# The gate products of a mixing layer: one block instead of five, low parts on GpSimd, four high buffers, gates through DRAM

## The chip, the cores and the metric

One core of a Trainium2 chip. The metric is the device time of one execution in microseconds; before the change the median of three runs is 4073.41 us (4073.11 to 4075.11). The profiled execution took 4088.57 us, of which its records span 4086.9.

## What is computed

The kernel runs two transformer blocks on 256 tokens of width 2048 in float32. The first ends in a layer of product-key experts, whose rows are gathered from DRAM. The second is a mixing layer and a feed-forward layer. The change is in the mixing layer of the second block:

```python
proj = h @ w_in                     # 2048 x (10240 + 16 + 3 * 2048); the last 6144 columns are the gates
o_sb  = stick_breaking_attention(rms(q_sb), rms(k_sb), v_sb)     # 6 heads of 128
o_dil = dilated_mixture(rms(q_dil), rms(k_dil), v_dil, slopes)   # 6 heads, three dilations, softmax over them
log_a = log_sigmoid(a_gla @ w_gla_a + b_gla_a) / 16
o_gla = rms(gla(q_gla, k_gla, v_gla, log_a)) * silu(r_gla)       # 4 heads, gated linear attention
g = sigmoid(gate_cols.reshape(b, t, 3, 2048))
y = g[:, :, 0] * (o_sb @ w_br_sb) + g[:, :, 1] * (o_dil @ w_br_dil) + g[:, :, 2] * (o_gla @ w_br_gla)
x = x + gate1 * (y @ w_out)
```

## The kernel before

**Slabs.** Every weight matrix is streamed from DRAM in slabs of 512 rows by 512 columns (1 MB, `ring`, four slots, loaded by SP's queue in the order of the program). A float32 product is made of three products of rounded operands: ScalarE writes a slab's rounded value (`high_part`, L336, 128x2048) into one of two buffers `slab_high`, a second engine subtracts it from the slab (`low_part`, L343), and TensorE multiplies high by high, low by high and high by low (24 matmuls a slab). For the slabs of the gates and of the branches the low part goes back into the slab's own ring slot (`ring_low`; `is_in_place`), so that slot is free only when TensorE has used the slab (`slot_free`). Semaphores count slabs: `landed`, `high_done`, `low_done`, `slabs_used`.

**Gates between the attention's products.** The 48 gate slabs (12 blocks of 512 columns, four slabs each) are independent of the attention. Five blocks of instructions in turn hold the attention (heads L1847, stick-breaking L1950, dilated L2066, gated linear L2221, branches L2431), and at chosen places of each engine's program the helpers `gate_loads`, `gate_highs`, `gate_lows` and `gate_slabs` put in the gate slabs up to a given number. TensorE makes 8 slabs by the end of the heads, 14 by the end of the stick-breaking part, 21, and 36; the last 12 follow at the head of the branch block. VectorE does all the attention's arithmetic and the low parts of the gate slabs, one at a time between its steps (`then` waits for the step before). Products of the gates go to the banks 6 and 7. After each fourth slab ScalarE takes them out with a sigmoid (L1808) into `staged`; SP writes nine of the twelve blocks to DRAM (`gate_rows`, L1789) and reads them back in three pieces (L2436); the last three stay in SBUF.

**The gated linear attention** goes over eight levels (`for lv in range(LV + 1)`, L2399): TensorE makes a level's products from `qe` and `ke`; VectorE scales these for the next level (L2289, L2290), masks and adds this level's products (L2306 to L2312), and forms the next exponents (L2283, L2285), of which ScalarE takes the exponential (L2354). TensorE made one gate slab between two levels.

**Branches.** 16 slabs, whose products with the attention's outputs are multiplied with the gates (L2489) and summed (L2494) into `y`.

Before this part stands the section `MIX` (the first 10240 columns of `w_in`), whose left operand is made by `final` and `normed` from the residual `res`. After it `transposed` and `gated_residual("mixer", ...)` multiply `y` with `w_out` and add to `res` (L2573). The gathers of the experts (L1668), long before, are issued by GpSimd, which copies 8 row numbers (L1661) for every 8 gathers, while VectorE works through the rows (L1515, L1529).

Of the kernel before, what the change touches and what calls it, by code (L numbers as in the profile page):

```python
# [9 lines left out]
F32 = mybir.dt.float32  # L10
# [19 lines left out]
def build(nc, a, out):  # L30
# [39 lines left out]
    with ctx:  # L70
# [39 lines left out]
        res_, _ = place_at("res", TT * D)  # L110
# [19 lines left out]
        low = low_[:, :].rearrange("p (s k n) -> p s k n", s=PARTS, k=KS)  # L130
        res, nat = view(res_[:, :], [TT, D]), view(nat_[:, :], [TT, D])
# [108 lines left out]

        def split_index(g):

            return g - whole_before[g]
# [84 lines left out]
        def high_part(act, g, i=None):  # L328

            n, up = split_index(g), 0 if i is None else i * 8  # L330
            act.wait_ge(landed[g % SLOTS], reach[g] if i is None else i * 32 + reach[g])
            if i is not None:
                act.wait_ge(slabs_used, up + (g - PARTS + 1))
            elif n >= PARTS:
                act.wait_ge(slabs_used, split_slabs[n - PARTS] + 1)  # L335
            nc.scalar.copy(high[:, n % PARTS], ring[:, g % SLOTS]).then_inc(high_done, 1)  # L336

        def low_part(eng, g, i=None):
# [4 lines left out]
            eng.tensor_tensor(dst, ring[:, g % SLOTS], high[:, n % PARTS].bitcast(F32), ALU.subtract)\  # L343
# [1066 lines left out]
        s_hi, s_lo = sem("mix_left_high"), sem("mix_left_low")  # L1410
        s_wa, s_ap = sem("rank_columns_landed"), sem("rank_products")
# [14 lines left out]
        with nc.Block() as block:  # L1426
# [255 lines left out]
            def _(sp):  # L1682
# [15 lines left out]
                sp.dma_start(shift_row, mods[0].rearrange("(k q) -> k q", q=P).partition_broadcast(P)).then_inc(s_shf, 16)  # L1698
                stream(sp, MIX)
                sp.wait_ge(s_wa, 80)  # L1700

# [74 lines left out]
        SPILLED = GATE_BLOCKS - 3  # L1776
        gate_rows = nc.dram_tensor("gate_rows", (SPILLED, P, TT * NB), F32, kind="Internal").ap()
        staged = spare[:, 3 * TT * NB:4 * TT * NB]
        last_gates = view(spare[:, 0:3 * TT * NB], [3, TT, NB])
        s_gate, s_spill = sem("gates_done"), sem("gates_spilled")  # L1780
        at = {"SP": 0, "PE": 0, "ACT": 0, "DVE": 0}

        def gate_loads(sp, end):

            for m in range(at["SP"], end):
                b = m // 4 - 1
                if m % 4 == 0 and 0 <= b < SPILLED:
# [5 lines left out]
        def gate_highs(act, end):  # L1793

            for n in range(at["ACT"], end):
                if n % 4 == 1 and 0 <= n // 4 - 1 < GATE_BLOCKS:
                    sigmoid(act, n // 4 - 1)
                high_part(act, gate0 + n)
            at["ACT"] = end

        def sigmoid(act, b):

            act.wait_ge(slabs_used, gate0 + 4 * b + 4)
            if 0 < b < SPILLED:
                act.wait_ge(s_spill, 16 * b)
            for t in range(TT):
                dst = staged[:, t * NB:(t + 1) * NB] if b < SPILLED else last_gates[:, b - SPILLED, t, :]
# [3 lines left out]
        def gate_lows(dve, end):  # L1811

            for n in range(at["DVE"], end):
                low_part(dve, gate0 + n)
            at["DVE"] = end
# [15 lines left out]
        def in_place_product(g, k, o, lh, ll, first, final):  # L1831

            hi = high[:, split_index(g) % PARTS, k, :]
# [3 lines left out]

        s_hs, s_hr, s_hn = sem("head_step"), sem("head_root"), sem("heads_normed")
# [8 lines left out]
        with nc.Block() as block:  # L1847
            @block.sync
            def _(sp):
                gate_loads(sp, 8)  # L1850

            @block.vector
            def _(dve):
                v = nc.vector
                n = [0]

                def then(ins, mark=None):
                    ins.then_inc(s_hs, 1)
                    n[0] += 1
                    hmarks[mark] = n[0]  # L1860
                    dve.wait_ge(s_hs, n[0])

                def copy_pair(m):
                    dve.wait_ge(s_hT, m + 1)
                    for j in range(2):
                        _, _, dst, hh, gcol = heads[2 * m + j]
                        src = ps[m % 4][:, j * T:(j + 1) * T]
                        if gcol is None:
                            last = v.tensor_scalar(dst[:, hh, :], src, P ** -0.5 if dst is gqT else 1.0, None, ALU.mult)
                        else:  # L1870
                            last = v.tensor_scalar(dst[:, hh, :], src, gains[:, gcol:gcol + 1], None, ALU.mult)
                    last.then_inc(s_hc[1], 1)

                gate_lows(dve, 1)
                copy_pair(1)
                copy_pair(3)
                for t in range(TT):
                    for i, qk in enumerate((sb_qk, dil_qk)):
                        hv = view(qk[:, t, :], [2 * SBH, HD])
                        then(v.tensor_tensor(sq, hv, hv, ALU.mult))  # L1880
                        then(v.tensor_reduce(qk_ss[:, t, i * 2 * SBH:(i + 1) * 2 * SBH], sq, AX, ALU.add))
                        gate_lows(dve, 2 + 2 * t + i)
                then(v.tensor_scalar(qk_ss, qk_ss, 1.0 / HD, EPS, ALU.mult, ALU.add), "ss")
                dve.wait_ge(s_hr, 1)
                then(v.reciprocal(qk_ss, qk_ss))
                for i, qk in enumerate((sb_qk, dil_qk)):
                    for t in range(TT):
# [828 lines left out]
```

## Time and profile before

| | |
|---|---|
| median of 3 runs | 4073.41 us |
| profiled execution, its span | 4088.57 us, 4086.9 us |
| TensorE busy | 2384.8 us, 58% of the span |
| VectorE busy | 2670.7 us, 65% |
| ScalarE busy | 809.8 us, 20% |
| GpSimd busy | 1152.0 us, 28%, nearly all before 2330 us |
| DMA, mean over the span | 252 GB/s |

All times in the views are microseconds from the start of the span unless they are marked ns. PE is TensorE, PEld its weight loads, DVE is VectorE, ACT is ScalarE, POOL is GpSimd, SP the engine that issues the loads. "L343" is a line of the kernel. A matmul's duration overlaps with the next one's; busy time doesn't count the overlap twice. The part that the change touches begins at 2697.5 us, when the first gate slab's high part starts, and ends at 3200.7 us, when the transposes of `y` start.

### The profile page before, as it was taken

The numbers are of one execution on the slowest core, as the hardware profiler recorded it, in microseconds if no ns is written. First come the engines' busy times: TensorE is split into PE (matmuls) and PEld (weight loads), VectorE is DVE, ScalarE is ACT, GpSimd is POOL, SyncE is SP. The second block draws the span as 40 slices with busy tenths as digits, with TensorE's granted clock in tenths as the row PEclk, the third lists the DMA queues.
The fourth block names the chain that finished last, engine by engine and source line by source line (L and its number), as shares of the span: only waits on it lengthen the run. The fifth ranks groups of instructions, "written<-read, shape, count | busy, mean of one in ns | idle before, by whom it ended". The sixth has DMA issues, their size and how long they took to land. (4 is left out here: it accounts for less than half of the span.)

```text
span 4086.9 us, 28912 instructions
## 1 busy us (share of the span) xinstructions
PE 2384.8 (58%) x10296; PEld 1784.6 (44%) x10296; DVE 2670.7 (65%) x2821; ACT 809.8 (20%) x679; POOL 1152.0 (28%) x605
## 2 busy tenths in 40 slices
PE   7798877870000000000000099998879969999999
PEld 4444436640000000000000088886668758888787
DVE  1876645367999988998888844456765544444444
ACT  1000113310000000000000033334433333333333
POOL 0000000005777888888888600000000000000000
PEclk9899978875555555555555599989989989999999
DMA  5255585669999999999999755533446545555554
GB/s 167 103 177 204 176 317 182 218 248 409 402 402 388 391 380 388 374 412 389 373 395 369 309 181 191 193 110 127 130 147 204 184 148 190 188 191 186 182 192 160
DMA packets 332247, 1029.49 MB, mean 252 GB/s; under 512 B 35256, under 2 KB 35768, under 8 KB 264696
## 3 DMA queue, kind: packets, MB, share of 16 engines
q1 hardware_dynamic: 258424, 491.31, 35.6%
q0 software_dynamic: 73728, 536.90, 32.8%
q8 instruction: 61, 1.00, 0.1%
q14 instruction: 34, 0.28, 0.0%
HBM read 1021.28 MB, written 6.86 MB: 252 GB/s over the span
## 5 line engine op out<-in xcount | busy, mean ns | idle before, releaser
L343 DVE TENSOR_TENSOR slab_low<-ring,slab_high 128x2048 fp32r<-128x2048 f32 x240 | 549.7, 2292 | 713.5 <-ACT slab_high L336 713.5
L336 ACT CAST slab_high<-ring 128x2048 fp32r<-128x2048 f32 x304 | 579.5, 1909 | 1051.7 <-PE bank L322 811.8
L1718 PE MATMUL bank<-ident,nat 128*128 128x128 f32 x32 | 8.9, 433 | 1300.7 <-DVE nat L1574 1300.7
L1529 DVE SCALAR_TENSOR_TENSOR res<-pool,res 128x2048 f32<-128x2048 f32 x256 | 603.2, 2356 | 81.1 <-DMA pool<-in_peer_v,small 52.5
L320 PE MATMUL bank<-slab_high,left_high 128*128 128x512 f32 x1568 | 616.3, 393 | 27.8 <-DVE slab_low L343 27.8
L1515 DVE CUSTOM_DVE_ANT_0 pool<-pool,nat 128x2048 f32<-128x2048 f32 x256 | 576.8, 2292 | 62.5 <-DMA pool<-in_peer_u,small 52.7
L321 PE MATMUL bank<-slab_low,left_high 128*128 128x512 f32 x1568 | 614.2, 392 | 0.0
L322 PE MATMUL bank<-slab_high,left_low 128*128 128x512 f32 x1568 | 613.8, 391 | 0.0
L1668 POOL DMA_INDIRECT pool<-in_peer_v,small x256 | 550.6, 2151 | 102.7 <-issue 68.3
L1718 PEld LDWEIGHTS bank<-ident,nat 128*128 128x128 f32 x32 | 5.7, 216 | 1304.6 <-DVE nat L1574 1304.6
L1668 POOL DMA_INDIRECT pool<-in_peer_u,small x256 | 501.6, 1960 | 153.8 <-issue 74.5
L320 PEld LDWEIGHTS bank<-slab_high,left_high 128*128 128x128 f32 x1568 | 297.1, 189 | 90.0 <-DVE slab_low L343 28.8
L322 PEld LDWEIGHTS bank<-slab_high,left_low 128*128 128x128 f32 x1568 | 296.9, 189 | 62.4
L321 PEld LDWEIGHTS bank<-slab_low,left_high 128*128 128x128 f32 x1568 | 297.2, 190 | 61.8
L311 PE MATMUL bank<-ring,left_scratch 128*128 128x512 f32 x640 | 277.9, 595 | 1.0 <-PEq L477 1.0
L1307 POOL IOTA small<- 128x16 f32 x1 | 0.1, 149 | 846.0 <-SPq L1304 846.0
L343 DVE TENSOR_TENSOR ring_low<-ring,slab_high 128x2048 fp32r<-128x2048 f32 x64 | 146.7, 2292 | 101.2 <-ACT slab_high L336 95.9
L1834 PE MATMUL bank<-slab_high,left_high 128*128 128x512 f32 x384 | 160.3, 418 | 55.8 <-DVE ring_low L343 42.9
L311 PEld LDWEIGHTS bank<-ring,left_scratch 128*128 128x128 f32 x640 | 121.7, 191 | 151.1 <-issue 151.1
L396 PE MATMUL bank<-ring,pool 128*32 128x512 f32 x768 | 122.5, 752 | 72.1 <-DMA ring<-in_w_ada 62.5
L1835 PE MATMUL bank<-ring_low,left_high 128*128 128x512 f32 x384 | 155.9, 406 | 0.0
L1836 PE MATMUL bank<-slab_high,left_low 128*128 128x512 f32 x384 | 155.8, 406 | 0.0
(494 smaller groups left out, 2877.8 us busy)
## 6 DMA issues: line engine op xcount, KB each, us to landing
ring<-in_w_in SPq DMA_DIRECT2D x148, 1024.0 KB, 5.1
ring<-in_w_ada SPq DMA_DIRECT2D x96, 1024.0 KB, 7.3
ring<-in_w_ffn_in SPq DMA_DIRECT2D x88, 1024.0 KB, 5.0
ring<-in_w_ffn_out SPq DMA_DIRECT2D x44, 1024.0 KB, 5.0
ring<-in_w_out SPq DMA_DIRECT2D x32, 1024.0 KB, 5.1
ring<-in_peer_wq SPq DMA_DIRECT2D x16, 1024.0 KB, 5.1
ring<-in_w_br_gla SPq DMA_DIRECT2D x8, 1024.0 KB, 5.0
gate_rows<-slab_low_scratch SPq DMA_DIRECT2D x9, 512.0 KB, 5.9
```

The costliest lines, as they stand in the source:

```text
L311: last = nc.tensor.matmul(o, raw_left[:, k0 + k, t * P:(t + 1) * P], ring[:, slot, k, :], start=start and k == 0, stop=stop and k == KS - 1)
L320: nc.tensor.matmul(o, lh, high[:, part, k, :], start=first, stop=False)
L321: nc.tensor.matmul(o, lh, low[:, part, k, :], start=False, stop=False)
L322: last = nc.tensor.matmul(o, ll, high[:, part, k, :], start=False, stop=final)
L336: nc.scalar.copy(high[:, n % PARTS], ring[:, g % SLOTS]).then_inc(high_done, 1)
L343: eng.tensor_tensor(dst, ring[:, g % SLOTS], high[:, n % PARTS].bitcast(F32), ALU.subtract)\
L1515: v.tensor_tensor_reduce(out=rows_[r], in0=rows_[r], in1=nat[:, t, :], scale=1.0, scalar=0.0, op0=ALU.mult, op1=ALU.add, accum_out=dots[:, ...
L1529: v.scalar_tensor_tensor(res[:, t, :], rows_[r], actv[:, t, bass.ds(i * GB + r, 1)], res[:, t, :], ALU.mult, ALU.add).then_inc(s_free, 1)
L1668: g.indirect_dma_start(rows_[r], None, src, bass.IndirectOffsetOnAxis(st[:, r:r + 1], 0))\
L1834: nc.tensor.matmul(o, lh, hi, start=first, stop=False)
L1835: nc.tensor.matmul(o, lh, ring_low[:, g % SLOTS, k, :], start=False, stop=False)
L1836: return nc.tensor.matmul(o, ll, hi, start=False, stop=final)
```

## The change

It leaves the arithmetic as it is, apart from where and when it is done:

- The five blocks become one. What each engine did in them are functions (`heads_on_tensor`, `stick_on_vector`, and so on) that are called in turn; new semaphores (`s_ol`, `s_gol`, waits for `s_hc` and others) replace the ends of the blocks.
- The low parts of all 64 in-place slabs are made by GpSimd (`gate_lows(g, ...)`) instead of VectorE.
- For these slabs there are four high buffers instead of two: the two of `slab_high` and two laid over `res`, which is written to DRAM before the `MIX` slabs and read back in the `mixer` block.
- All 48 gate slabs are made between the attention's products; the table `BEFORE` says how many slabs TensorE has made before each step. ScalarE goes four slabs further (`+ DEEP`) before each of its steps.
- All 12 blocks of gate products go to DRAM, as plain copies of the banks; they come back in four pieces, and the sigmoid is taken then, one of 128x3072 for each.

```diff
+        DEEP = 2 * PARTS
+        def high_of(g):
+            if is_in_place(g):
+                slot = (g - first_slab[GATES]) % DEEP
+                return high[:, slot] if slot < PARTS else over_res[:, slot - PARTS]
+            return high[:, split_index(g) % PARTS]
...
+            elif is_in_place(g) and g - first_slab[GATES] >= DEEP:
+                act.wait_ge(slabs_used, g - DEEP + 1)
+            elif is_in_place(g) and g - first_slab[GATES] >= PARTS:
+                act.wait_ge(s_away, 16)
...
+                sp.wait_ge(s_res, 4 * TT)
+                sp.dma_start(residual_rows, res_[:, :]).then_inc(s_away, 16)
                 stream(sp, MIX)
...
-        SPILLED = GATE_BLOCKS - 3
+        BEFORE = {"h4": 4, "h8": 6, "h12": 8, "sa": 8, "sb": 12, "sc": 16, "da": 16, "db": 20, "dc": 22, "ga": 24,
+                  "gb": 25, "gc": 28, "g1": 28, "g2": 30, "g3": 32, "g4": 34, "g5": 36, "g6": 38, "g7": 40, "g8": 42,
+                  "go": 44, "gt": 46}
...
-            for n in range(at["ACT"], end):
-                if n % 4 == 1 and 0 <= n // 4 - 1 < GATE_BLOCKS:
-                    sigmoid(act, n // 4 - 1)
+            for n in range(at["ACT"], min(end, IN_PLACE)):
+                if n % 4 == 3 and 0 <= n // 4 - 1 < GATE_BLOCKS:
+                    take_gate(act, n // 4 - 1)
                 high_part(act, gate0 + n)
...
-                last = nc.scalar.activation(dst, ps[6 + t][:, :], ACT.Sigmoid)
+                last = nc.scalar.copy(staged[:, t * NB:(t + 1) * NB], ps[6 + t][:, :])
...
+            for m in (4, 8, 12):
+                gate_highs(act, BEFORE[f"h{m}"] + DEEP)
+                copy_pair(m)
+                copy_pair(m + 2)
...
+        def stick_on_scalar(act):
+            gate_highs(act, BEFORE["sa"] + DEEP)
+            act.wait_ge(s_ss, sm["abs"])
...
+            gate_highs(act, BEFORE["sc"] + DEEP)
+            for h in range(SBH):
+                act.wait_ge(s_so, h + 1)
+                nc.scalar.copy(oTh[:, h, :], ps[h][:, 0:T]).then_inc(s_oc, 1)
...
+        def gla_on_gpsimd(g):
+            gate_lows(g, BEFORE["db"])
+            g.wait_ge(s_mk, 4)
+            g.wait_ge(s_so, SBH)
+            g.wait_ge(s_ds, dk["max"])
+            g.memset(upto[:, :], 1.0).then_inc(s_gi, 1)
...
+            for lv in range(1, LV + 1):
+                gate_highs(act, BEFORE[f"g{max(lv - 1, 1)}"] + DEEP)
+                act.wait_ge(s_gs, gm[f"diff{lv}"])
+                nc.scalar.activation(ee, ee, ACT.Exp).then_inc(s_gf, 1)
...
+            gate_loads(sp, B0 + 1)
+            sp.wait_ge(s_gs, gm["out"])
+            for n in (0, 1, 3):
+                read_back(n)
+            sp.wait_ge(s_gT2, 4)
+            read_back(2)
+            gate_loads(sp, IN_PLACE)
...
+        def branch_on_scalar(act):
+            gate_highs(act, B0 + 4)
+            for nb in range(OB):
+                act.wait_ge(s_back[nb], 16)
+                nc.scalar.activation(sg[nb], sg[nb], ACT.Sigmoid).then_inc(s_sg, 1)
+                gate_highs(act, B0 + 4 * nb + 8)
+
+        def branch_on_gpsimd(g):
+            gate_lows(g, IN_PLACE)
...
+                    if residual_away:
+                        sp.dma_start(res_[:, :], residual_rows).then_inc(s_away, 16)
```

## Rows read from the trace of the kernel before

**Rows 1.** Busy times by stretch: busy us (count) of each engine, TensorE's granted clock, DMA.

```profile
2697.50:2759.60 62.10, 55.45 (x256) 45.88 (x256) 47.66 (x39) 27.97 (x32) 0.00 (x0) 0.93 0.42 137
2759.60:2821.70 62.10, 49.10 (x252) 41.16 (x253) 35.51 (x32) 25.93 (x21) 0.89 (x4) 0.92 0.35 113
2821.70:2887.00 65.30, 54.17 (x246) 44.47 (x246) 40.90 (x62) 26.83 (x43) 0.53 (x2) 0.92 0.40 129
2887.00:2911.70 24.70, 23.14 (x102) 18.12 (x102) 14.18 (x17) 13.76 (x11) 0.87 (x4) 0.93 0.53 169
2911.70:2994.00 82.30, 64.28 (x328) 54.09 (x328) 78.91 (x77) 27.25 (x23) 0.00 (x0) 0.96 0.33 106
2994.00:3039.00 45.00, 31.32 (x137) 25.34 (x136) 26.78 (x22) 18.38 (x17) 0.00 (x0) 0.87 0.38 118
3039.00:3110.20 71.20, 68.59 (x289) 55.92 (x290) 27.51 (x12) 22.93 (x15) 0.00 (x0) 0.96 0.69 243
3110.20:3200.70 90.50, 87.32 (x385) 71.82 (x384) 59.03 (x47) 29.64 (x17) 0.00 (x0) 1.00 0.57 192
```

**Rows 2.** TensorE's waits from 2697 to 3201: us in total, times, longest.

```profile
PE bank L1834 <- DVE ring_low L343: 42.9, 13, 10.0
PE bank L1834 <- ACT slab_low_scratch L1808: 9.5, 6, 2.9
PE bank L1834 <- PEq L2221: 3.4, 1, 3.4
```

**Rows 3.** Groups of instructions, 2697 to 3110: low and high parts, exponentials and their tables.

```profile
L343 DVE TENSOR_TENSOR ring_low<-ring,slab_high 128x2048 fp32r<-128x2048 f32 x49 | 112.3, 2292 | 72.5 <-ACT slab_high L336 67.4 <-PEq L2221 4.3
...
L336 ACT CAST slab_high<-ring 128x2048 fp32r<-128x2048 f32 x49 | 93.1, 1905 | 181.8 <-PE bank L1836 157.7 <-PEq L1426 24.0
...
L2354 ACT ACTIVATE slab_low_scratch<-slab_low_scratch 128x1024 f32<-128x1024 f32 x8 | 8.5, 1057 | 4.5 <-DVE slab_low_scratch L2285 4.5
...
L2354 ACT ACT_TABLE_LOAD x2 | 2.6, 1283 | 0.0
```

**Rows 4.** DMA issues, 2690 to 3215: size of one, us to landing.

```profile
ring<-in_w_in SPq DMA_DIRECT2D x44, 1024.0 KB, 5.0
...
pool<-gate_rows SPq DMA_DIRECT2D x3, 1536.0 KB, 8.6
```

**Rows 5.** Busy times while two read-backs and a slab are under way.

```profile
3052.00:3056.00 4.00, 4.00 (x19) 3.31 (x18) 0.97 (x1) 1.91 (x1) 0.00 (x0) 1.00 1.03 417
```

**Rows 6.** GpSimd's copy of 8 numbers, and two of the 64 beside VectorE's timeline.

```profile
L1661 POOL COPY small<-pool x64: 187/1770/2183, 919.0 to 2298.0; 128x8 uint32 x62, 128x8 uint32<-128x8 uint32 x2
...
2032.47 2.35 DVE L1529 SCALAR_TENSOR_TENSOR res<-pool,res 128x2048 f32<-128x2048 f32 x1 [0.43 <-DMA pool<-in_peer_v,small]
...
2032.86 2.00 POOL L1661 COPY small<-pool 128x8 uint32 x1
...
1308.06 2.29 DVE L1494 TENSOR_REDUCE pool<-left_scratch 128x128 f32<-128x2048 f32 x1
...
1310.08 0.20 POOL L1661 COPY small<-pool 128x8 uint32 x1
```

**Rows 7.** GpSimd's own operations, whole span.

```profile
L430 POOL MEMSET pool<- 128x1024 f32 x1 | 1.0, 951 | 0.3 <-POOLq L2705 0.3
...
L441 POOL TENSOR_SCALAR_AFFINE_SELECT causal<-causal 128x128 f32<-128x128 f32 x1 | 0.3, 288 | 0.0
...
L443 POOL TENSOR_SCALAR_AFFINE_SELECT small<-small 128x8 f32<-128x8 f32 x1 | 0.2, 188 | 0.0
```

**Rows 8.** Groups, 2697 to 3110: attention's work on VectorE, ScalarE, TensorE.

```profile
L2283 DVE TENSOR_TENSOR slab_low_scratch<-slab_low_scratch 128x1024 f32<-128x1024 f32 x8 | 9.8, 1225 | 0.3
...
L2312 DVE TENSOR_TENSOR pool<-pool,slab_low_scratch 128x1024 f32<-128x1024 f32 x7 | 8.6, 1226 | 0.2
...
L2330 DVE TENSOR_TENSOR pool<-pool,small 128x2048 f32<-128x2048 f32 x1 | 2.3, 2291 | 0.0
...
L1908 ACT ACTIVATE pool<-bank,small 128x256 f32<-128x256 f32 x6 | 2.4, 478 | 0.0
...
L2399 PE MATMUL bank<-pool 128*128 128x128 f32 x120 | 14.7, 275 | 0.0
...
L1936 PE MATMUL bank<-ident,pool 128*128 128x128 f32 x64 | 9.4, 310 | 0.5 <-PEq L1426 0.5
```

More of the change, by code:

```diff
@@ L342, in low_part @@
             dst = ring_low[:, g % SLOTS] if is_in_place(g) else low[:, n % PARTS]
-            eng.tensor_tensor(dst, ring[:, g % SLOTS], high[:, n % PARTS].bitcast(F32), ALU.subtract)\
+            eng.tensor_tensor(dst, ring[:, g % SLOTS], high_of(g).bitcast(F32), ALU.subtract)\
                .then_inc(low_done, 1)
@@ new lines, in heads_on_tensor @@
+        def heads_on_tensor(pe):
+            for m in range(len(heads) // 2):
+                src = heads[2 * m][0]
+                if m and m % 4 == 0:
+                    gate_slabs(pe, BEFORE[f"h{m}"])
+                if src is not gla_qk:
+                    pe.wait_ge(s_hn, 1 if src is sb_qk else 2)
+                if m >= 4:
+                    pe.wait_ge(s_hc[m % 2], (m - 4) // 2 + 1)
+                for j in range(4):
+                    src, h, *_ = heads[2 * m + j // 2]
+                    t = j % 2
+                    last = nc.tensor.transpose(ps[m % 4][:, j * P:(j + 1) * P], src[:, t, h * P:(h + 1) * P],
+                                               ident[:, :])
+                last.then_inc(s_hT, 1)
+            gate_slabs(pe, BEFORE["sa"])
@@ new lines, in build @@
+        y = nat
+        sg = [view(pool[:, at_:at_ + 3 * TT * NB], [3, TT, NB]) for at_ in (0, 3 * TT * NB, T2_at)]
+        sg.append(view(spare[:, 0:3 * TT * NB], [3, TT, NB]))
+        ytmp = view(pool[:, 6 * TT * NB:7 * TT * NB], [TT, NB])
+        assert 7 * TT * NB <= oT_at and OB == 4
+        s_ga, s_free_bank, s_sg = sem("gated_steps"), sem("branch_products_taken"), sem("gates_squashed")
+        s_back = [sem(f"gates_read_back{n}") for n in range(OB)]
+        ends = [sum(br_rows[:i + 1]) - 1 for i in range(3)]
@@ new lines, in branch_on_scalar, with branch_on_vector, then, gate @@
+        def branch_on_scalar(act):
+            gate_highs(act, B0 + 4)
+            for nb in range(OB):
+                act.wait_ge(s_back[nb], 16)
[3 more added lines that the diff above has]
+            gate_lows(g, IN_PLACE)
+        def branch_on_vector(dve):
+            v = nc.vector
+            n = [0]
+            def then(ins):
+                ins.then_inc(s_ga, 1)
+                n[0] += 1
+                dve.wait_ge(s_ga, n[0])
+            def gate(nb, i):
+                dst, u = y[:, :, nb * NB:(nb + 1) * NB], 3 * nb + i
+                dve.wait_ge(slabs_used, gate0 + B0 + 4 * nb + ends[i] // KS + 1)
+                dve.wait_ge(s_sg, nb + 1)
+                for t in range(TT):
+                    last = v.tensor_tensor((dst if i == 0 else ytmp)[:, t, :], ps[u % 4 * TT + t][:, :],
+                                           sg[nb][:, i, t, :], ALU.mult)
+                last.then_inc(s_free_bank, 1)
+                dve.wait_ge(s_free_bank, u + 1)
+                if i:
+                    then(v.tensor_tensor(dst, dst, ytmp, ALU.add))
+            for nb in range(OB):
+                gate(nb, 0)
+                gate(nb, 1)
+                gate(nb, 2)
```

1060 lines of the change are left out of this document (489 added, 571 removed).

## The prediction

> **What bounds the kernel now.** I read the windows view first, cut at the ends of the blocks that the change touches [rows 1]. From 2697.5 to 3110.2 us, TensorE works on the 48 gate slabs and on the attention's own products; it is busy 346.1 of 412.7 us (the first seven rows). In the eighth row, the branch products, it is busy 87.3 of 90.5 us: 16 slabs, 87.3 / 16 = 5.46 us a slab, and that is the floor of every slab here. TensorE's granted clock is 0.87 to 0.96 in the seven stretches and 1.00 in the eighth; the missing shares, each times its stretch, add up to 28 us of full-speed time, of which 346/413, some 23 us, fell on busy time. So 48 slabs cost 48 x 5.46 = 262 us, and 346 - 23 - 262 = 61 us are the attention's products. The floor of this part is 323 us and it takes 413: 90 us are open, 67 idle and 23 at the lower clock level.
>
> Next I read what TensorE waits for [rows 2]. The longest entry is the low part on VectorE (42.9 us in 13 waits), then the sigmoid that empties the gates' two banks (9.5 us). The end of a block costs 2.3 to 3.4 us; one of four such rows is shown, 11.2 us together. VectorE makes 49 low parts in this part (one belongs to slab 48), 112.3 us at 2.292 each [rows 3], out of 271.5 us busy (sum of the first seven rows of rows 1). It is the engine that is late: in the stretch 2911.7 to 2994.0 it is busy 78.9 of 82.3 us.
>
> Outside this part nothing that sets the end is changed, so the sum is made here.
>
> **The change part by part.**
>
> (1) *Removed.* The 48 + 16 low parts leave VectorE, and with them the 42.9 us of waits; the four block ends inside go (11.2 us). The bank is now emptied by a copy. Nearly every end of a four-slab group now lies beside attention products, so most of the 9.5 us goes too. The most that all this can give is the 90 us above.
>
> (2) *Waits that the new order makes.* A slab has a fixed loop: its ring slot is free when TensorE has used the slab four before it, the load lands 5.0 us later [rows 4], ScalarE needs 1.9 us for the high part [rows 3]. So the high part of slab g+4 is ready 7.1 us (with 0.2 for the hand-overs) after TensorE has ended slab g. ScalarE now runs its high parts up to four slabs ahead of what it does for the attention, and what is queued behind them waits for this loop:
> - The last head copies stand behind the high part of slab 11, which needs slab 7: 7.1 + 4 x 0.48 for the copies, against 16 of the 64 transposes, 2.3 us [rows 8]. TensorE idles 6.7 us.
> - The stick-breaking outputs stand behind the high part of slab 19, which needs slab 15: 7.1 and the first copy, against the four microseconds of the output products, some 3.8 us (an estimate: 36 small products at the pace of those in [rows 8]).
> - The dilated softmax has four slabs of cover (21.8 us) and its scores' products (some 5) where it had more. Its own VectorE work in the third stretch is 40.9 - 7 x 2.29 = 24.9 us, about 20 of it before the weights are ready, and ScalarE's is about 13: 33 against 27, 6 to 8 idle; I take 7.
> - Between level 0 and level 1 of the gated linear attention there is no slab any more. The exponential waits for the high part of slab 31: 7.1 + table load and function (1.3 + 1.1) [rows 3] + two scalings (2 x 1.22) [rows 8] = 11.9, against some 6 us of products and copies (the cumulative sum's, and 2.0 of level 0: 14.7 + 2.1 us of L2399 over 8.5 levels, its larger row in [rows 8]). TensorE idles 6; a level before it another 1 to 2.
> - The end of that attention: copies of 2.5 us, two squares and two sums of 1.22, three products of 2.29 [rows 8] and a root of about 1, 15 to 16 us, against two slabs (10.9): 4.7.
> - First slab later (GpSimd's low part takes longer) and gate banks: 2.9 + 3.2.
> Together 37 us. Then the branch part: all four read-backs (1.5 MB each) are put into SP's queue between slab 52 and slab 53. Two read-backs and a slab now run at 417 GB/s [rows 5]; at that, 4 x 1.57 + 2 x 1.05 MB are 20 us, and a single read-back's 8.6 us from issue to landing [rows 4], against 3.8 for its bytes, says that some latency comes on top, 3 us; then 1.9 + 4.5 of high and low part. Slab 53 is ready 30 us after slab 48, TensorE reaches it after 22 to 24: 6.5 idle, and 2 for slab 52, whose high part stands behind the first sigmoid. 8.5 us, where before had none. Idle stretches are followed by the lower clock, as now; for about eight stalls I count 10 to 12 us against the 23 of before.
>
> (3) *GpSimd's low part.* No row shows a two-input operation of 128x2048 there. One input and one output grows from 0.188 us (128x8) to 0.288 (128x128) [rows 7], 0.83 ns an element, 1.9 us for 2048; a fill alone is 0.93 ns an element. If the two reads pass one after the other under the write it is 3.5 us, if all three passes add up 5.2. I take the middle, 4.4, and 4.5 from start to start. That is below 5.46, so GpSimd alone keeps pace: after a slab, 5.0 + 1.9 + 4.5 and the hand-overs = 11.6 us to the next in its slot, against 16.4 of three slabs. The Trainium skill, "GPSIMD Engine Reference", section 3.1, gives 4497 ns for a tensor_tensor of 2048 fp32 and 2293 on VectorE, whose row here is 2292; the sum would be the same.
>
> Without any contention this gives: 323 (floor) + 37 + 11 = 371 us instead of 413, and 8.5 more in the branches: 4086.9 - 42 + 8.5 = 4053 or, with the walk slab by slab, which lets some stalls overlap less, 4050 to 4055: **34 us faster**.
>
> (4) *The port between VectorE and GpSimd.* [rows 6] show GpSimd's copy of 8 elements a row, in the gathers' loop. It takes 187 ns at best, but the median of 64 is 1770. The two pairs of lines tell why: beside a scalar_tensor_tensor with two operands in SBUF the copy ends at 2034.86, 0.04 us after VectorE's operation (2032.47 + 2.35 = 2034.82); beside a tensor_reduce, with one operand, it takes 0.20. I take it that the two cannot read at once, and that the one that comes second waits for the whole instruction of the first. The gathers show only short GpSimd reads, so no row shows VectorE waiting; between none of it and all of it I take all, as the direction that rows show is of that kind.
>
> The Trainium skill, "SBUF — State Buffer", section "Who interferes with whom", says the lock works both ways, for a VectorE instruction with two SBUF inputs against a GpSimd one that reads SBUF. By that rule a change of this kind works against itself, and the time is that of the forecast; the trace agrees in the direction that it shows.
>
> The price, if it works both ways, from rows: VectorE's operations of two SBUF operands in this part add up to about 96 us; per level of the gated linear attention there are six, 4 x 1.22 + 1.23 + 0.29 = 6.4 us (two of these rows in [rows 8]). 48 low parts are 216 us; 216 + 96 = 312, which would just fit. But per level two slabs need 9.0 + 6.4 = 15.4 us of the port, and with the hand-overs 16, where TensorE needs 2 x 5.46 + 2.0 = 12.9: seven levels, 22 us. Elsewhere each dependent step of VectorE's chain can find one subtraction in front: heads, two more on the path (9 us); stick-breaking, three steps and two lows more (10); dilated, one (4.5); up to level 1, one or two (5); the end, two (8). 58 us together. Where VectorE's next operation is already queued it may keep the port; for that I take 6 off: 52 us.
>
> (5) *Residual.* 2 MB go out before the slabs of the `MIX` section and come back in the `mixer` block. The write stands before slab 4's load, but 22 us of prefetched slabs cover its 6 to 8 us; the read back has 20 us until the first addition. Nothing, and up to 3 us if that cover is short.
>
> **The sum.** 4086.9 - 34 + 52 = 4105 us of span. The profiled execution took 4088.57, its span 4086.9; the median of the runs is 4073.41, 15 lower. Carried over to the median: 4073.4 + 18 = **4091 us**. About 0.2% (8 us) can be told from no change.
>
> **The rivals.**
> - *The port is shared finely* or GpSimd's instruction doesn't hold it against VectorE. Then (4) is nearly free and the time is 4073 - 34 = 4039. For it: only the other direction is in rows. Against it: the copies of [rows 6] wait for the whole of an instruction, which no fine sharing would make them do. 0.28.
> - *Exclusive, but the slabs prepared ahead absorb it.* Four high buffers let GpSimd run four slabs ahead, and it works while VectorE waits for ScalarE. Only the port's total counts, and half of the 52 us go: 4065. 0.12.
> - *GpSimd is the bound.* If its low part takes 5.2 us or more, all three passes in a row, 48 x 0.8 = 38 us come on top: 4129. It decides from the point where the subtraction and VectorE's share exceed 5.46 us a slab. 0.1.
> - Forecast, 0.5, its own range 4068 to 4115.
> That the change doesn't do what it says is no case here: the low parts are issued on GpSimd by name, and no order is left to a planner.
>
> **How the numbers follow.** Faster by over 0.2%: the first rival (nearly all of 0.28) and half of the second, 0.34. Within: the rest of the second and the low end of the forecast, 0.12. Slower: 0.54. The range goes from 4032 (the first rival with its stalls a little shorter) to 4122 (between the forecast's end and GpSimd as the bound).
>
> **What would show each step.** The mean of the GpSimd subtraction, and whether it stretches by whole VectorE operations. The durations of VectorE's two-operand operations in the levels, or the idle time before them: 1.22 us each now; waits of up to 4.4 us mean exclusive. The distance from level to level: 16 us forecast, 12.9 in the first rival. TensorE's wait before the stick-breaking scores (6.8), before level 1, and before slab 53, where the low part is late because of the load. Wrong is the prediction if the levels lie 13 us apart and VectorE's operations are as long and as dense as now.

## The result, and the profile of the changed kernel

| | before | changed |
|---|---|---|
| median | 4074.26 us | 4106.53 us (4101.85 to 4108.3) |
| ratio | | 1.0077, 95% interval 1.006 to 1.0094 |
| span of the profiled execution | 4086.9 us | 4100.1 us |
| first head transposes to the transposes of `y` ("the stretch") | 2697.5 to 3200.7, 503.2 us | 2683.5 to 3212.55, 529.0 us |
| after the stretch | 886.2 us | 887.5 us |

The changed kernel is 32 us slower; a second comparison of the same two (below) gave 17. In the profiles the stretch is 26 us longer the first time and 24 the second, and what follows it is as long as before within 1.5 us. The two spans differ by less, because the changed kernel's stretch happens to begin 14 us earlier; what lies ahead of it scatters (last section).

Busy times of the changed kernel by stretch, cut where TensorE starts the stick-breaking scores, the dilated scores, the transposes ahead of the gated linear attention, level 1, level 8, the branch products (columns as in [rows 1]):

```profile
2683.50:2756.47 72.97, 56.85 (x256) 47.30 (x257) 50.57 (x30) 30.12 (x34) 60.95 (x18) 0.87 0.38 130
2756.47:2831.53 75.06, 63.06 (x300) 54.10 (x300) 32.71 (x22) 28.26 (x22) 40.53 (x9) 0.89 0.37 126
2831.53:2900.10 68.57, 58.96 (x271) 50.04 (x272) 38.47 (x64) 21.81 (x42) 33.67 (x11) 0.88 0.34 115
2900.10:2943.43 43.33, 29.34 (x143) 23.30 (x142) 19.32 (x17) 18.87 (x15) 27.36 (x6) 0.92 0.46 155
2943.43:3060.78 117.35, 100.05 (x448) 84.15 (x449) 97.98 (x59) 34.43 (x26) 58.02 (x13) 0.90 0.39 132
3060.78:3111.20 50.42, 42.25 (x192) 35.65 (x193) 31.96 (x23) 17.51 (x16) 29.34 (x6) 0.93 0.38 132
3111.20:3212.55 101.35, 89.61 (x386) 73.10 (x385) 35.48 (x32) 39.35 (x21) 65.87 (x14) 0.97 0.67 239
```

The row to look at is the fifth, the levels: VectorE is busy 98.0 of 117.4 us, although its low parts are gone. The groups of the whole stretch say with what. First GpSimd's low parts, then VectorE's own operations (mean ns of one behind the busy time):

```profile
L360 POOL TENSOR_TENSOR ring_low<-ring,slab_high 128x2048 fp32r<-128x2048 f32 x32 | 157.1, 4919 | 132.7 <-ACT slab_high L353 132.7
L360 POOL TENSOR_TENSOR ring_low<-ring,residual_parts 128x2048 fp32r<-128x2048 f32 x32 | 156.7, 4909 | 49.3 <-ACT residual_parts L353 49.3
```

```profile
L2295 DVE TENSOR_SCALAR pool<-pool 128x128 f32<-128x128 f32 x7 | 22.8, 3254 | 0.2
...
L1907 DVE TENSOR_TENSOR pool<-pool,small 128x1536 f32<-128x1536 f32 x4 | 19.8, 5020 | 0.0
...
L1899 DVE TENSOR_TENSOR slab_low_scratch<-pool 128x1536 f32<-128x1536 f32 x4 | 16.6, 4142 | 0.1
...
L1998 DVE TENSOR_TENSOR pool<-pool,causal 128x768 f32<-128x768 f32 x2 | 10.4, 5234 | 0.0
...
L2298 DVE TENSOR_TENSOR slab_low_scratch<-bank,pool 128x512 f32<-128x512 f32 x14 | 9.0, 686 | 0.2
...
L1900 DVE TENSOR_REDUCE small<-slab_low_scratch 128x12 f32<-128x1536 f32 x4 | 7.0, 1753 | 0.1
```

An operation on 128x128 elements takes 3254 ns. It reads one operand, and that lies in SBUF. Operations with one of two operands in a bank (L2298) are as short as they were, and so is the reduce (L1900), which has one operand in SBUF too. In the stretch VectorE is busy 306.5 us in 244 operations; the same 244 take 189.7 us in a kernel below whose GpSimd reads nothing. So some 117 us of what is recorded as VectorE's work is waiting inside the operations. One level, GpSimd's line first, then VectorE's:

```profile
3006.71 9.59 POOL L360 TENSOR_TENSOR ring_low<-ring,residual_parts 128x2048 fp32r<-128x2048 f32 x2 [8.21 <-ACT residual_parts L353]
...
3006.12 1.22 DVE L2280 TENSOR_TENSOR pool<-nat,slab_low_scratch 128x1024 f32<-128x1024 f32 x1
3007.37 4.46 DVE L2295 TENSOR_SCALAR pool<-pool 128x128 f32<-128x128 f32 x1
3011.86 4.60 DVE L2296 SCALAR_TENSOR_TENSOR pool<-pool 128x128 f32<-128x128 f32 x1
3016.49 1.29 DVE L2298 TENSOR_TENSOR slab_low_scratch<-bank,pool 128x512 f32<-128x512 f32 x2
```

GpSimd's first subtraction is issued at 3006.71 while L2280 runs, waits for its end (3007.34), and works till 3011.8. The mask operation of 0.23 us, issued 0.03 us after L2280, gets through only then. By that time GpSimd's second subtraction stands there and goes first, and the next mask operation (0.29 us) waits 4.3 us again. The pair ends at 3016.30, the mask operation at 3016.46. Both directions of the exclusion are in these lines. What TensorE waits for, in the stretch:

```profile
PE bank L2383 <- DVE pool L2280: 27.3, 7, 10.0
PE bank L1856 <- POOL ring_low L360: 11.5, 3, 6.4
PE bank L2170 <- DVE slab_low_scratch L2129: 9.6, 1, 9.6
PE bank L2040 <- DVE pool L1998: 8.4, 1, 8.4
PE bank L2402 <- DVE pool L2320: 8.2, 1, 8.2
PE bank L2033 <- ACT pool L1923: 6.7, 1, 6.7
PE bank L1950 <- DVE pool L1907: 6.5, 1, 6.5
PE bank L2163 <- DVE mixed_low L2010: 3.6, 1, 3.6
PE bank L1856 <- ACT slab_low_scratch L1830: 2.4, 1, 2.4
```

The 42.9 us of [rows 2] for the low part on VectorE are gone, and of the 9.5 us of bank waits 2.4 are left. In their place stand waits for attention steps of VectorE, 60 us (first, third to fifth and seventh row).

### The profile page after: what moved, and what is told of

It reads as the page before. It is cut to its first block and busy times, and to the rows that moved or that the text cites. A ratio compares the mean times of both kernels' runs of the same rounds, so it can differ in the third digit from the quotient of the medians.

```text
span 4100.1 us, 28858 instructions
## 1 busy us (share of the span) xinstructions
PE 2386.0 (58%) x10296; PEld 1787.1 (44%) x10296; DVE 2646.2 (65%) x2757; ACT 807.5 (20%) x674; POOL 1457.8 (36%) x669
## 5 line engine op out<-in xcount | busy, mean ns | idle before, releaser
L353 ACT CAST slab_high<-ring 128x2048 fp32r<-128x2048 f32 x272 | 518.2, 1909 | 943.7 <-PE bank L335 811.7
L333 PE MATMUL bank<-slab_high,left_high 128*128 128x512 f32 x1568 | 615.8, 393 | 27.5 <-DVE slab_low L360 27.5
L335 PE MATMUL bank<-slab_high,left_low 128*128 128x512 f32 x1568 | 613.4, 391 | 0.0
L360 POOL TENSOR_TENSOR ring_low<-ring,slab_high 128x2048 fp32r<-128x2048 f32 x32 | 157.1, 4919 | 132.7 <-ACT slab_high L353 132.7
L360 POOL TENSOR_TENSOR ring_low<-ring,residual_parts 128x2048 fp32r<-128x2048 f32 x32 | 156.7, 4909 | 49.3 <-ACT residual_parts L353 49.3
L333 PE MATMUL bank<-slab_high,hidden_high 128*128 128x512 f32 x352 | 138.3, 393 | 7.1 <-DVE slab_low L360 7.1
```

Of the source, the lines that this page charges most:

```text
L333: nc.tensor.matmul(o, lh, high[:, part, k, :], start=first, stop=False)
L335: last = nc.tensor.matmul(o, ll, high[:, part, k, :], start=False, stop=final)
L353: nc.scalar.copy(high_of(g), ring[:, g % SLOTS]).then_inc(high_done, 1)
L360: eng.tensor_tensor(dst, ring[:, g % SLOTS], high_of(g).bitcast(F32), ALU.subtract)\
```

## The experiments

**Theory:** GpSimd's subtraction and VectorE's operations on two SBUF operands shut each other out for whole instructions, and this costs more than the low parts cost on VectorE. **Rival A:** the new order costs the time (high parts ahead, read-backs in one heap), whoever makes the low part. **Rival B:** only the sum of the time at the port (the way to SBUF that the two engines can't use at once) counts, not how long one instruction is. Each run but the changed kernel and before has one profile. Of each run: the stretch as above, the distance between levels as the mean of seven from level 1 to level 8 (starts of TensorE's level products), and the kernel against the runs of before beside it. Before has no entry for the level, because TensorE makes one slab between two levels there and two here. The mean hides an unevenness: in the changed kernel the first two of the seven take 14.2 and 14.1 us and the other five 17.8, which is the number that some of the expectations name.

| run | GpSimd per slab | level, us | stretch, us | median minus before | ratio, 95% |
|---|---|---|---|---|---|
| before | nothing | | 503.2 | | |
| changed | one subtraction | 16.8 | 529.0 | +32 | 1.006 to 1.0094 |
| changed, again | the same | 16.5 | 527.0 | +17 | 1.0025 to 1.0054 |
| e1_vector_lows | nothing | 15.9 | 500.8 | -2 | 0.9983 to 1.0013 |
| e2_fill_only | two fills | 13.4 | 473.1 | -32 | 0.9907 to 0.9945 |
| e9_copy_only | two copies | 13.8 | 481.2 | -26 | 0.9926 to 0.9961 |
| e3_four_pieces | four quarters | 15.0 | 503.9 | -1 | 0.9983 to 1.0005 |
| e10_two_pieces | two halves | 15.9 | 508.1 | 0 | 0.9993 to 1.0012 |
| e4_masks_early | one subtraction | 15.9 | 524.2 | +22 | 1.0035 to 1.0073 |
| e5_order | one subtraction | 16.4 | 509.8 | +11 | 1.0015 to 1.0039 |
| e7_all | four quarters | 14.5 | 482.9 | -20 | 0.9938 to 0.997 |
| e8_vector_tuned | nothing | 13.6 | 468.7 | -34 | 0.989 to 0.9931 |
| e11_finer | nothing | 13.8 | 463.8 | -43 | 0.9878 to 0.9914 |

**The changed kernel again** (`c_after`), as the measure for the others:

> The changed kernel once more, unchanged, beside the next three, so that they can be compared with it on the same chip. Stretch 529 us, 26 more than before; kernel 25 to 33 us above the kernel before. If the stretch repeats within 1 us while the whole varies by several, the rest of the difference is the scatter of what lies ahead of the stretch.

The stretch was 527.0 us, 2 less than the first time; the kernel stood 16.8 us above before, not 25 to 33.

**Low parts back on VectorE.** Each low part stands just before the step that TensorE needs after its slab, for instance in the levels:

```diff
                     exponents(lv + 1)
+                gate_lows(dve, 28 + 2 * lv)
                 dve.wait_ge(s_gT, lv + 1)
...
         def branch_on_gpsimd(g):
-            gate_lows(g, IN_PLACE)
+            return
```

> The changed kernel with its 64 low parts back on VectorE, each just before the step that TensorE needs after that slab; one block, four high buffers, the new order of slabs, the read-backs and the late sigmoids stay. Port theory (what costs time is that GpSimd's subtraction and VectorE's two-operand operations shut each other out): VectorE's operations fall back to their old lengths (the mask operation of 0.23 us, now 4.45, back to 0.23), a level takes two low parts (4.6) + its own 6.4 + some 3 us of waiting for ScalarE, 14 us instead of 17.8; the stretch from the first head transposes to the transposes of y, 529 us now, becomes 495 to 510, the kernel 4070 to 4085 us. Rival (the new order and the waits for the high parts ahead cost the time, whoever makes the low part): 525 us or more, 4100 us and above.

The stretch was 500.8 us: 26 to 28 us of the change's cost are gone with GpSimd alone. The level came to 15.9 us, not 14, since both low parts of a level stand in one place and TensorE waits some 4 us in every second level. So rival A is out as the main cause. But the order's waits are there: 7.0 us before the stick-breaking scores, 3.75 before the dilated ones, 5.7 before level 1. I take them, with the 37.6 us that TensorE still waits for low parts, for the reason why this kernel is no faster than before, though it has as many low parts and fewer block ends; the last two candidates below bear this out.

**GpSimd writes, but reads nothing.** It keeps the place and nearly the length of the work, and takes away the reads alone.

```diff
-            eng.tensor_tensor(dst, ring[:, g % SLOTS], high_of(g).bitcast(F32), ALU.subtract)\
-               .then_inc(low_done, 1)
+            if is_in_place(g):
+                eng.memset(dst.bitcast(F32), 0.0).then_inc(s_fill, 1)
+                eng.wait_ge(s_fill, g - first_slab[GATES] + 1)
+                eng.memset(dst.bitcast(F32), 0.0).then_inc(low_done, 1)
...
```

> The changed kernel with GpSimd's low part replaced by two fills of the same tile one after the other: GpSimd is busy about as long (2 x 1.9 us) and writes, but reads nothing. Left out: the low parts of the 64 slabs are zero, so the products lack them; the number of products is the same. Port theory: without reads VectorE is not held up, its operations are as long as before the change; level to level 13 to 14 us, the stretch 470 to 480 us instead of 529, the kernel 4045 to 4060 us. Rival (the order's waits): the stretch stays at 520 or more; 4098 us and above. A third case: also a write of GpSimd holds VectorE up: then the mask operations stay at 2 us and longer.

Measured: 4048.28 us against 4080.28, the stretch 473.1. This is the change nearly without contention. The first of the two fills, and two VectorE groups; the last is the mask operation, which was at 3254:

```profile
L361 POOL MEMSET ring_low<- 128x2048 f32 x64 | 116.1, 1813 | 203.5 <-ACT slab_high L353 137.3 <-ACT residual_parts L353 66.2
...
L2281 DVE SCALAR_TENSOR_TENSOR slab_low_scratch<-slab_low_scratch 128x1024 f32<-128x1024 f32 x8 | 9.8, 1225 | 0.3
...
L2301 DVE TENSOR_SCALAR pool<-pool 128x128 f32<-128x128 f32 x7 | 2.2, 317 | 0.2
```

And what TensorE still waits for, the same view as for the changed kernel:

```profile
PE bank L1862 <- POOL ring_low L363: 9.7, 3, 6.0
PE bank L2039 <- ACT pool L1929: 6.9, 1, 6.9
PE bank L1862 <- ACT slab_low_scratch L1836: 5.8, 5, 2.9
PE bank L2389 <- DVE pool L2286: 5.6, 1, 5.6
PE bank L2408 <- DVE pool L2326: 4.5, 1, 4.5
PE bank L2176 <- DVE slab_low_scratch L2135: 4.3, 1, 4.3
PE bank L2169 <- DVE mixed_low L2016: 3.7, 1, 3.7
```

These are the waits that the order makes, by themselves. One reservation: the two fills take 3.6 us a slab where the subtraction takes 4.5, so this run also has 0.9 us less of GpSimd's time.

And the fills are not free of contention altogether. The mask operation has a mean of 317 ns here, against 227 where GpSimd is idle. Six of the seven met the end of a fill and took 325 to 341 ns, until it was over; the seventh met none and took 228. A fill whose end lay further off shows it better:

```profile
2868.41 1.81 POOL L363 MEMSET ring_low<- 128x2048 f32 x1
2868.47 0.29 DVE L2256 SCALAR_TENSOR_TENSOR pool<-pool,causal 128x128 f32<-128x128 f32 x1
2868.79 1.51 DVE L2257 TENSOR_SCALAR pool<-pool 128x128 f32<-128x128 f32 x1
```

The operation with two operands takes its 0.29 us inside the fill. The one with a single operand, 0.23 us by itself, ends at 2870.30, 0.08 us after the fill. All eight `tensor_scalar` operations from SBUF to SBUF that met a fill, and a cast of one operand, were held until its end, while the scalings of two operands (1.22 us) never were. So a GpSimd instruction that only writes does hold VectorE up, which is the third case of the expectation, but it holds these operations of one operand and not those of two. In this run that is 3 to 4 us of VectorE's time.

**GpSimd reads one operand.**

```diff
...
+                eng.tensor_copy(dst, high_of(g).bitcast(F32)).then_inc(s_fill, 1)
+                eng.wait_ge(s_fill, g - first_slab[GATES] + 1)
+                eng.tensor_copy(dst, high_of(g).bitcast(F32)).then_inc(low_done, 1)
...
```

> The changed kernel with GpSimd's low part replaced by two copies of the high part, one after the other: one operand is read and one written. Left out: the low parts are wrong (a copy of the high part), the products are as many. By the fills (no read, stretch 473 us) and the slope of GpSimd's one-operand rows (about 1.9 us for 2048) a pair takes about 3.8 us. If a single read is enough to shut VectorE out, its two-operand operations stretch by up to 1.9 us each, as with pieces of that length, and the stretch is 500 to 515 us. If it takes two operands on GpSimd's side too, VectorE's operations are as short as with the fills and the stretch is 473 to 477 us.

The stretch was 481.2 us, between the two expectations: neither held. In the trace one read is enough to shut VectorE's two-operand operations out (GpSimd's lines, then VectorE's):

```profile
2948.49 1.90 POOL L361 CAST ring_low<-slab_high 128x2048 fp32r<-128x2048 f32 x1 [1.88 <-ACT slab_high L353]
2950.45 2.77 POOL L363 CAST ring_low<-slab_high 128x2048 fp32r<-128x2048 f32 x1
...
2949.62 1.83 DVE L2307 TENSOR_TENSOR pool<-pool,slab_low_scratch 128x1024 f32<-128x1024 f32 x1
2951.49 2.80 DVE L2279 TENSOR_TENSOR slab_low_scratch<-slab_low_scratch 128x1024 f32<-128x1024 f32 x1
```

The addition of 1.22 us, issued at 2949.62, ends at 2951.45, so it ran from 2950.23, as the first copy came to its end (2950.39). The second copy, issued 0.06 us after that, ends at 2953.22, one copy's length behind the addition. The next VectorE operation, 1.22 us too, ends at 2954.29. In these lines the two engines alternate, instruction by instruction. But a copy holds the port for 1.9 us, the pair for 3.8 instead of 4.5, and all this costs only 8 us over the fills. The Trainium skill, "SBUF — State Buffer", section "Who interferes with whom", states just this pair of facts: a VectorE instruction with two SBUF inputs contends with a GpSimd one that reads SBUF, and not with one that only writes it. These two runs agree (1225 ns beside fills, 1.83 and 2.80 us beside copies); for the operations of one operand that the fills held, see above.

**The low part in pieces.**

```diff
...
+            for c in range(pieces):
+                last = eng.tensor_tensor(dst[:, c * w:(c + 1) * w], ring[:, g % SLOTS, c * w:(c + 1) * w],
+                                         high_of(g)[:, c * w:(c + 1) * w].bitcast(F32), ALU.subtract)
+            last.then_inc(low_done, 1)
```

> The changed kernel with each GpSimd low part cut into four instructions of 512 elements a row. If the port is held for one whole instruction at a time, a VectorE operation that finds GpSimd there waits at most 1.2 us instead of 4.6, the mask operations fall from 4.5 to 1.5 us or less, a level from 17.8 to 14.5 us, the stretch from 529 to about 500, the kernel to 4075 to 4085 us. Rival (only the sum of both engines' time at the port counts, and GpSimd's four fixed costs come on top): no gain, 4105 us or up to 5 more. Rival (waits of the order): 4105.

> The changed kernel with each low part in two pieces of 1024. Whole, the stretch is 527 to 529 us, in four pieces 504, with nothing read 473. If what a VectorE operation waits is the rest of one GpSimd instruction, the half lies between: about 513 to 517 us, and the mask operations wait up to 2.3 us. Rival (four pieces helped for another reason, such as the place where GpSimd gives way): 525 us.

The same subtraction, undisturbed, takes 4.5 us whole, 2.39 in halves and 1.27 in quarters, so pieces make GpSimd's work longer, 4.8 and 5.1 us a slab. The stretch nevertheless fell from 527 to 508 and 504 us (the halves were expected at 513 to 517). Rival B, that the sum alone counts, falls with this: the same subtraction in 0.3 and 0.6 us more, and a stretch that is 19 to 25 us shorter. (Whether the extra time holds the port isn't shown; if it doesn't, the time there is the same, and the rival still forecasts no gain.) Over the fills' 473 us the pieces still cost 35 and 31 us. The levels alone, from level 1 to level 8, follow the length of one instruction: 21 to 23 us over the fills for the whole subtraction, 17 for halves, 10.5 for quarters, 2.5 for the copies of 1.9 us. Outside them quarters are no better than halves: TensorE waits 11.3 us for low parts in the heads with quarters, 6.6 with halves, 2.2 with the fills. The mask operation of the four-piece kernel, 909 ns now:

```profile
L2299 DVE TENSOR_SCALAR pool<-pool 128x128 f32<-128x128 f32 x7 | 6.4, 909 | 0.2
```

**The masks early.** The two small operations that the subtractions hit go ahead of VectorE's wait for the level's products.

> The changed kernel with the two small mask operations of each level moved ahead of VectorE's wait for the level's products, so that they run while it would idle. Today the two low parts of a level hold up just these two (4.5 us each, for 0.23 and 0.29 us of work), on the chain exponents - exponential - scaling - masks - masked products - sum - exponents. If the port wait follows the place in the order, the chain loses up to 9 us and finds some of it elsewhere: a level 15 us instead of 17.8, 15 to 20 us over seven levels, the kernel 4087 to 4092 us. Rival (the low parts then hold up the scalings or the masked products for the same time): within 3 us of the changed kernel.

The gain was 3 to 5 us, nearly the rival's. The masks are short again, and the first operation of the exponents, 1958 ns in the changed kernel, has their wait:

```profile
L2273 DVE TENSOR_TENSOR slab_low_scratch<-slab_low_scratch 128x1024 f32<-128x1024 f32 x8 | 32.8, 4103 | 0.3
```

Here, in a chain of dependent steps, the lock found another step.

**Two waits of the order taken away.**

```diff
-                gate_highs(act, BEFORE[f"h{m}"] + DEEP)
+                gate_highs(act, BEFORE[f"h{m}"] + (DEEP if m < 12 else 2))
...
-            for n in (0, 1, 3):
-                read_back(n)
+            read_back(0)
+            gate_loads(sp, B0 + 2)
+            read_back(1)
+            gate_loads(sp, B0 + 4)
             sp.wait_ge(s_gT2, 4)
             read_back(2)
+            gate_loads(sp, B0 + 5)
+            read_back(3)
```

> The changed kernel with two of the waits of its order taken away: ScalarE makes the last head copies ahead of the high parts of slabs 10 and 11, and the four read-backs stand between the loads of slabs 52 to 56, one at a time. Low parts stay on GpSimd. If waits of the order and port waits simply add up: 6.7 us less before the stick-breaking scores and 6 to 8 us less at slabs 52 and 53, the stretch 515 us instead of 529. Rival (the port is what sets the pace, and a wait taken away comes back at the next step): 523 us or more, at most 6 us gained.

The stretch was 509.8 us, 17 less than the changed kernel beside it (expected 14). TensorE's wait before the stick-breaking scores fell from 6.6 to 1.1 us, the one before slab 53 from 6.0 to nothing. These two make 11.5 us; the other 5 are TensorE's busy time, 433.5 us against 438.8, at a granted clock of 0.93 against 0.91. The waits of the order and those for the port simply add up. So rival A is not wrong, it is a second, smaller term.

> e5_order, with the low parts in four pieces of 512 and the masks early as well. Four pieces alone gave 504 us for the stretch where the changed kernel has 529; with the two waits of the order gone 490 to 493 us if they add up, kernel 10 to 14 us below the kernel before; 500 or more if they don't. Of the early masks I expect 0 to 3 us here, since their port wait is short already.

The four edits together gave 482.9 us, 7 better than expected, and 4054.13 us: the change with GpSimd's low parts can be made 20 us faster than before.

**The candidate without GpSimd.** The low parts are back on VectorE and the two waits of the order are gone, both as above; in addition (shown in part):

```diff
-            gate_highs(act, BEFORE["sc"] + DEEP)
+            gate_highs(act, BEFORE["sc"] + 3)
...
                     then(v.tensor_tensor(acc, acc, mtmp, ALU.add), f"level{lv}")
+                    gate_lows(dve, 29 + 2 * lv)
```

> The candidate without GpSimd: low parts on VectorE, but each a slab or more ahead of its need (in a level one while ScalarE makes the exponential, one after the sum), the two waits of the order gone, and the high parts before the stick-breaking outputs and before level 1 shortened by one or two slabs so that those steps don't wait for a load. The low parts on VectorE in the changed kernel's order gave 501 us for the stretch. From that: 7 (heads) + 3.8 (outputs) + 5.7 (level 1) + 4 (slab 49 and on) + half of the 30 us of waits for low parts = 465 to 480 us; kernel 20 to 35 us below the kernel before. Rival (VectorE's own chain is the bound of the levels: two low parts of 2.3, 6.4 of its own and 2.4 of waiting make 13.4 to 14 us a level anyway): 485 to 492 us.

> The candidate e8_vector_tuned with two low parts moved on VectorE: that of slab 4 goes from behind all four scalings of the heads to behind the first two (TensorE waits 3.7 us for it), and of the two low parts in the dilated scores one goes behind the maximum, where VectorE waits for the exponentials anyway (TensorE waits 9.8 us for the softmax). If the waits are what they look like, 3.7 + 2.3 to 4.6 us less: the stretch 461 to 463 us instead of 469, the kernel 38 to 41 us below the kernel before. Rival (the waits return at the next step): 468 us.

Measured 468.7 and 463.8 us for the stretch, 4040.18 and 4031.19 us for the kernels. The first expectation held; the second named 461 to 463 us, and the stretch came out 1 us above that. The last is 43 us below the kernel before (1.04%). Its levels are 13.8 us apart with all low parts on VectorE; with the low parts spread over two places in the level, TensorE waits nearly as little there as with GpSimd's fills, which was what the change hoped for. What is left of TensorE's waits there:

```profile
PE bank L1856 <- DVE ring_low L360: 11.6, 8, 2.9
PE bank L2407 <- DVE pool L2298: 6.4, 1, 6.4
PE bank L2426 <- DVE pool L2343: 6.3, 1, 6.3
PE bank L2186 <- DVE slab_low_scratch L2142: 2.8, 1, 2.8
```

## Why the prediction was right

Forecast +18 us, measured +32 and +17, and +26 and +24 in the stretch; the likeliest case was the one that came. Part of how near the size came is luck, as (4) shows.

**(1) and (2), without contention: -34 forecast; -30 in the stretch, -32 in the median of the fills.** Term by term, forecast and measured with the fills: stick-breaking scores 6.7 and 6.9; stick-breaking outputs 3.8 and 3.7; dilated softmax 7 and 4.3; level 1 6 and 5.6, before level 0 1 to 2 and 1.6; end of the gated linear attention 4.7 and 4.5; slab 53 6.5 and 6.0, slab 52 2 and 1.6. The loop of 5.0 + 1.9 + 0.2 us from a slab's end to the high part four slabs on stands in the trace of the fills: slab 7's last product ends at 2740.43 us, slab 11's high part at 2747.55, 7.1 us later, and it is 6.9 and 7.1 for slabs 15 and 27. e5_order confirms it by taking two of the waits away. (The terms of (2) before the branches add up to 35 or 36 us, not 37, unless the upper ends are taken.) The banks were counted with 3.2, and are 5.8. The mis-sized term is the slower clock: TensorE's busy time is 427.7 us with the fills against the floor of 323 + 87.3 = 410.3, 17 us where 10 to 12 were forecast. That alone would cover the 4 us that are missing.

**(3) 4.4 us for the low part, taken between 3.5 and 5.2.** Undisturbed it takes 4.5 to 4.6. The Trainium skill's 4497 ns ("GPSIMD Engine Reference", section 3.1) agrees. The mean of 4.91 contains waits. GpSimd as the bound (the third rival) doesn't show: in the levels it is busy 58.0 of 117.4 us.

**(4) Exclusive in both directions, +52 forecast; +56 in the stretch** (529.0 against 473.1 us with the fills, of which a part may be the fills' 0.9 us less of work a slab). The direction that no row of before showed is the one in the lines of the level above. By part, forecast and difference between the changed kernel and the fills: heads 9 and 8.6, stick-breaking 10 and 12.4, dilated 4.5 and 5.9, up to level 1 5 and 2.3, levels 22 and 23.2, end 8 and 3.6, branches none and 0. The level, forecast 16 us from 9.0 + 6.4 and hand-overs, was 16.8 and 16.5 in the mean. But it isn't that sum that sets it: the sum gives the same for every level, where the trace has 14.1 and 17.8; and halves, with 9.6 us of subtraction, gave 15.9 us, quarters with 10.2 gave 15.0, less than their own 10.2 + 6.4. What costs is the whole instruction in front of a dependent step, as the forecast had it for the other parts; that the sum came near in the levels is partly luck. Part of the price is the clock once more: TensorE is busy 440.1 us in the changed kernel against 427.7 with the fills. The granted clock is 0.91 on average in the stretch, against 0.95 with the fills and 0.94 in the kernel before. So 12 of the 56 us come as slower products, and 44 as idle time. The forecast had 52 us (58 before 6 were taken off) of idle time alone and nothing for the clock in this term, so two misses cancel. The 6 us taken off for operations already queued have no support: the second of two subtractions overtook an operation of VectorE that followed 0.03 us behind its predecessor. Nor did it help to be queued without waiting for the step before: the second of the two scalings, next to its predecessor in VectorE's program, takes a mean of 2061 ns beside the copies, 1218 beside the fills.

**(5) The residual: nothing, and that is what it is.** From the start of the last 16 transposes ahead of the section `MIX` to the head transposes it is 359.86 us before and 359.85 to 359.96 in eleven profiles of kernels that have the write, 356.85 in the changed kernel's first profile. After the stretch it is 886.2 before and 885.5 to 887.7 in all the others.

**The rivals.** Fine sharing was given 4039 and 0.28. The fills, which are this case made by hand, came to 32 us below before, that is 4042. So the price of the rival was right, and its mechanism fell. "Exclusive but absorbed" fell too: four high buffers didn't help, since TensorE waits 60 us for VectorE's chain and 11.5 for the low parts.

## What to carry to other kernels

Before work is moved to GpSimd, list what VectorE runs beside it that has two operands in SBUF, and above all how long its chain of dependent steps is: each step can wait for one whole GpSimd instruction, however short it is itself. Count the `tensor_scalar` operations and casts from SBUF to SBUF too: here they waited even for an instruction that only wrote. If the work must go there, cut it into pieces and keep reads out of it. And look first at where the moved work stood: here 48 low parts on VectorE were no obstacle, two in one place in front of a needed step were, and an order with them one slab ahead gave more than the second engine did.

## What was unexpected

- The size of an operation doesn't protect it: a `tensor_scalar` with one operand of 128x128 in SBUF, 0.23 us, waited like the two-operand ones and was recorded with 4.46 us. The reduce over 1536 elements with one operand never waited (1753 ns in all kernels). The prediction had counted two-operand operations only. The fills show that a single-operand `tensor_scalar` is the more exposed of the two kinds: it waits for a write alone.
- The wait is recorded inside the operation's duration, not as idle time before it. VectorE looked 117 us busier than it was.
- The price is not proportional to the time that GpSimd reads: quarters read longest and cost 31 us, halves 35, the whole 54 to 56, two copies (3.8 us a slab) 8. That less time at the port lets each level stay near TensorE's own 13.4 us is my reading of the copies; no run separates it.
- With unchanged code ahead of it, the stretch began anywhere from 2671.0 to 2698.1 us in the profiles of the changed kernel and its variants, and at 2697.5 in the one of before. So one profile's span says little about a change of 30 us. The length of the stretch is steadier: the two profiles of the changed kernel gave 529.0 and 527.0 us. Of the kernel before there is one profile. Why the first comparison gave +32 and the second +17, with stretches that differ by 2, stays open, and so does what makes the start of the stretch scatter.
